# Evictions as a stream of their own, one unit behind their matmuls, in a two-block transformer kernel

## The reference, cut to what matters

```python
# first block, 2 layers, 256 tokens
h = rmsnorm(x, norm_w); proj = h @ w_in            # 1024 -> 4360 columns
ya = softmax_attention(8 heads, causal, ALiBi) * silu(ag)
yb = head_norm(retention(4 heads, rotated q, k)) * silu(bg)
yc = head_norm(mlstm(4 heads, chunks of 128) * sigmoid(co)) * silu(cg)
x = x + concat(ya, yb, yc) @ w_out
...
# second block, 2 layers, x (256 tokens) and a context (256 tokens), 9 modulation vectors
x = x + 0.5 * m[2] * swiglu(modulate(rms_norm(x), m[0], m[1]), w_ffn1)      # and the context
z = modulate(rms_norm(x), m[3], m[4]) @ w_in                                # and the context
ya, yb = neighborhood_attention(6 heads), window_attention(6 heads, 2 kv)   # local and context keys
yc = silu(layer_norm(depthwise_conv(31 taps)))
x = x + m[5] * ((g0 * ya @ w_out_a + g1 * yb @ w_out_b + g2 * yc @ w_out_c) @ w_out)
x = x + 0.5 * m[8] * swiglu(modulate(rms_norm(x), m[6], m[7]), w_ffn2)      # hidden width 2816
```

## Time and profile before

| | |
|---|---|
| median of 3 runs | 2630.19 us (2627.18 to 2636.57) |
| the profiled execution | 2638.58 us, span 2636.8 us |
| PE busy | 2457.2 us, 93% of the span |
| DVE busy | 1600.4 us, 61% |
| ACT busy | 877.7 us, 33% |
| mean granted clock of PE | 0.945 of full speed |

### The profile page before, as it was taken

One profiled execution on the slowest core, in us unless ns is written; L12 is line 12 of the kernel. 1 busy time (PEld: TensorE's weight loads), 2 busy tenths in 40 slices (PEclk: granted clock), 3 DMA queues, 4 the chain that ended last, 5 costly groups with the idle time before them and its releaser, 6 DMA issues.

```text
span 2636.8 us, 33057 instructions
## 1 busy us (share of the span) xinstructions
PE 2457.2 (93%) x13210; PEld 2077.3 (79%) x13210; DVE 1600.4 (61%) x2950; ACT 877.7 (33%) x1488; POOL 222.6 (8%) x321
## 2 busy tenths in 40 slices
PE   5888887799999999989989999989999999998998
PEld 5777776688888876668888888888888887788998
DVE  3875875577767445554458986654443345665665
ACT  3343433322222333333332222232222234344443
POOL 1000000100001200001111111100000020011000
PEclk9898987799999897999989999989999989798999
DMA  6533542254444310112325655522322232134553
GB/s 227 180 121 104 175 136 72 75 173 168 168 167 152 96 62 22 37 54 86 101 80 192 237 210 203 191 85 88 100 93 95 96 104 84 52 121 152 183 184 122
DMA packets 95353, 332.99 MB, mean 126 GB/s; under 512 B 11040, under 2 KB 13216, under 8 KB 94816
## 3 DMA queue, kind: packets, MB, share of 16 engines
q1 hardware_dynamic: 70496, 244.41, 27.2%
q0 software_dynamic: 23376, 84.80, 10.0%
q10 hardware_dynamic: 1328, 1.66, 0.2%
HBM read 329.78 MB, written 2.48 MB: 126 GB/s over the span
## 4 chain that ended last, share of the span: by engine, by line
PE 77%; DVE 13%; ACT 5%; issue 3%; POOL 1%; DMA 1%; ACTq 0%; POOLq 0%; DVEq 0%
PE PS L417 76%; DVE WL L1083 3%; ACT WH L794 2%; DVE ST L1096 1%; DVE NT L1092 1%; PE PS L720 1%; ACT P L795 1%; DVE AR L1093 1%; DVE JK L1093 1%; DVE HL L1092 1%; DVE PJ L1092 1%; DVE CV L1092 1%; ACT PT L794 1%; POOL SS L1672 1%; DMA CST<-in_cst 0%
## 5 line engine op out<-in xcount | busy, mean ns | idle before, releaser
L417 PE MATMUL PS<-HH,WH 128*128 128x512 f32 (+1 forms) x2136 | 772.3, 362 | 21.7 <-DVE HL L1092 21.4
L1083 DVE TENSOR_TENSOR WL<-RAW,WH 128x1024 fp32r<-128x1024 f32 (+2 forms) x482 | 575.4, 1194 | 324.7 <-ACT WH L794 323.6
L417 PE MATMUL PS<-HL,WH 128*128 128x512 f32 (+1 forms) x2136 | 758.9, 355 | 0.0
L417 PE MATMUL PS<-HH,WL 128*128 128x512 f32 (+1 forms) x2136 | 758.8, 355 | 0.0
L794 ACT ACTIVATE WH<-RAW 128x1024 fp32r<-128x1024 f32 (+2 forms) x482 | 490.4, 1019 | 247.5 <-PE PS L417 247.5
L417 PEld LDWEIGHTS PS<-HH,WH 128*128 128x128 f32 x2136 | 415.1, 194 | 95.1 <-DVE HL L1092 28.6
L417 PEld LDWEIGHTS PS<-HL,WH 128*128 128x128 f32 x2136 | 416.0, 195 | 56.4
L417 PEld LDWEIGHTS PS<-HH,WL 128*128 128x128 f32 x2136 | 415.2, 194 | 56.8
L417 PE MATMUL PS<-GH,WH 128*128 128x512 f32 (+1 forms) x776 | 270.8, 349 | 0.0
L417 PE MATMUL PS<-GH,WL 128*128 128x512 f32 (+1 forms) x776 | 270.7, 349 | 0.0
L417 PE MATMUL PS<-GL,WH 128*128 128x512 f32 (+1 forms) x776 | 270.5, 349 | 0.0
(11 more groups left out here) (219 smaller groups left out, 3125.1 us busy)
## 6 DMA issues: line engine op xcount, KB each, us to landing
RAW<-in_wst SPq DMA_DIRECT2D x420, 512.0 KB, 3.5
AR<-in_w_adaT POOLq DMA_DIRECT2D x144, 512.0 KB, 3.7
RAW<-in_wst SPq DMA_DIRECT2D x48, 384.0 KB, 3.0
BM<-rpb_rows POOLq DMA_DIRECT2D x48, 64.0 KB, 2.6
CB<-in_cc POOLq DMA_DIRECT2D x2, 1024.0 KB, 9.9
RAW<-in_wst SPq DMA_DIRECT2D x8, 256.0 KB, 2.7
RAW<-in_wst SPq DMA_DIRECT2D x4, 396.0 KB, 5.3
rpb_rows<-in_rpb POOLq DMA_DIRECT2D x2, 697.5 KB, 10.0
```

The lines of the kernel that those rows point to most:

```text
L417: return e.matmul(o, l, r, start=start, stop=stop)
L1083: return e.tensor_tensor(out=o, in0=a, in1=b, op=op)
```

## The change

Four things change. (1) Evictions leave the D stream and become a stream V of their own on ACT, DVE and POOL. (2) A dense unit is written in two halves on PE; D therefore stands twice as often in `order` and the other streams are mixed between halves. ACT and DVE do `high` and `low` at the first half and nothing at the second. (3) The V step of unit e is put right after the first half of unit e+1, so behind the `high` and `low` of that step; a mark "F", and the first step of each norm, bring all evictions of finished units at once. (4) `boundary` has a new order written in halves, and the last M steps of a layer's projections stand behind an F.

```diff
@@ mix
     for name, n in steps.items():
+        if name == "D":
+            n *= 2
         out += [((2 * i + 1) / (2 * n), name) for i in range(n)]
@@ plan, first block
-        order += mix(D=2, A=3, M=4)
+        order += mix(D=2, A=3, M=2) + ["F", "M", "M"]
@@ boundary
         if last:
-            return ["D", "N", "D", "N", "N", "N", "N", "D"] + ["N"] * 5 + ["D"]
-        return ["N", "N", "D"] + mix(D=1, N=8) + ["D"] * HELD
+            return ["D", "N", "D", "D", "N", "N", "D"] + ["N"] * 2 + ["D"] + ["N"] * 3 + ["D", "N", "N", "D"]
+        return ["N", "D", "N", "D", "N", "N", "D", "N", "N", "D", "N", "N", "D", "N", "N"] + ["D", "D"] * HELD
@@ mixer
-        out += mix(B=nb - b0, P=4, C=9)
+        out += ["F"] + mix(B=nb - b0, P=4, C=9)
@@ plan, end
-    B = ["D"] * HELD
+    B = ["D", "D"] * HELD
...
+    out, dense, left, norm = [], 0, 0, 0
+    for name in order:
+        if name == "F" or name == "N" and norm % 10 == 0:
+            while left < dense // 2:
+                out.append("V")
+                left += 1
+        norm += name == "N"
+        if name == "F":
+            continue
+        out.append(name)
+        if name == "D":
+            dense += 1
+            if dense % 2 and left < dense // 2:
+                out.append("V")
+                left += 1
+    order = out + ["V"] * (len(S) - left)
@@ tensor_program, dense
+                todo = [(j, k) for j in range(len(x.tiles)) for k in range(un.kt)]
-                for j, d in enumerate(x.tiles):
+                for y, (j, k) in enumerate(todo):
+                    d = x.tiles[j]
+                    if y == len(todo) // 2:
+                        yield
@@ scalar_program (vector_program alike, with low(u); pool_program's dense() becomes evictions())
         def dense():
-            silu = [0]
             for u in range(NS):
                 high(u)
+            for x in S:
+                for u in x.split:
+                    high(u)
+                yield
+                yield
+
+        def evictions():
+            silu = [0]
             for e_ in S:
                 un = U[e_.u]
-                for u in e_.split:
-                    high(u)
                 for d in e_.tiles if un.last else ():
```

More of the change, by code:

```diff
@@ L465, in dense @@
                 u, un = x.u, U[x.u]
+                todo = [(j, k) for j in range(len(x.tiles)) for k in range(un.kt)]
                 wh = WH[:, u % NS, 0:un.kt * un.cols].rearrange("p (k c) -> p k c", c=un.cols)
                 wl = WL[:, u % NS, 0:un.kt * un.cols].rearrange("p (k c) -> p k c", c=un.cols)
-                for j, d in enumerate(x.tiles):
-                    if un.first:
+                for y, (j, k) in enumerate(todo):
+                    d = x.tiles[j]
+                    if y == len(todo) // 2:
+                        yield
+                    if k == 0 and un.first:
                         released(T[d].before)
-                    if j == 0:
+                    if y == 0:
                         q.wait_ge(*ad.at("wh", u))
@@ L474, in dense @@
                     P = PS[T[d].bank]
[L475 to L488, removed]
+                    a, z = un.first and k == 0, un.last and k == un.kt - 1
+                    c = slice(128 * j, 128 * j + 128)
+                    if un.mode == "f":
+                        xh, xl = operand(un, k, T[d].halves)
+                        m = T[d].cols
+                        mm(P[:, 0:x.n], wh[:, k, c], xh[:, m], a, False)
+                        mm(P[:, 0:x.n], wh[:, k, c], xl[:, m], False, False)
+                        i = mm(P[:, 0:x.n], wl[:, k, c], xh[:, m], False, z)
+                    else:
+                        xh, xl = operand(un, k, range(x.n // 2))
+                        mm(P[:, 0:un.cols], xh[:, c], wh[:, k, :], a, False)
+                        mm(P[:, 0:un.cols], xl[:, c], wh[:, k, :], False, False)
+                        i = mm(P[:, 0:un.cols], xh[:, c], wl[:, k, :], False, z)
+                    if k < un.kt - 1:
+                        continue
                     if x.closes and d == x.tiles[-1]:
@@ L1075, in scalar_program @@
         q.wait_ge(d_cst, 32)
-        return dict(D=dense(), N=norm(), M=mlstm(), T=retention(), A=attention1(), B=attention2(), L=lnorm(), E=ada())
+        return dict(D=dense(), N=norm(), M=mlstm(), T=retention(), A=attention1(), B=attention2(), L=lnorm(), E=ada(), V=evictions())
     def vector_program(e):
@@ L1109, in dense, with evictions @@
         def dense():
-            silu = [0]
             for u in range(NS):
                 low(u)
+            for x in S:
+                for u in x.split:
+                    low(u)
+                yield
+                yield
+        def evictions():
+            silu = [0]
             for e_ in S:
                 un = U[e_.u]
-                for u in e_.split:
-                    low(u)
                 for d in e_.tiles if un.last else ():
@@ L1664, in vector_program @@
         return dict(D=dense(), N=norm(), M=mlstm(), T=retention(), A=attention1(), B=attention2(), P=rope(), C=conv(),
-                    L=lnorm(), E=ada(), K=misc())
+                    L=lnorm(), E=ada(), K=misc(), V=evictions())
     def pool_program(e):
@@ L1683, in add, with evictions @@
             gn.same("ss", j, i, halves[-1])
-        def dense():
+        def evictions():
             for e_ in S:
@@ L1783, in misc @@
                 yield
-        return dict(D=dense(), N=norm(), M=mlstm(), T=retention(), L=lnorm(), E=ada(), K=misc())
+        return dict(V=evictions(), N=norm(), M=mlstm(), T=retention(), L=lnorm(), E=ada(), K=misc())
     def sync_program(e):
```

## The result

The changed kernel is slower: 2648.1 us (median of 6 runs, 2644.4 to 2653.8) against 2634.8 (6 runs of the kernel before, 2627.2 to 2644.6). The ratio is 1.005, interval 1.0026 to 1.0075. The forecast was 2614.7. The direction is wrong. The time lies near the edge of the range, and nearest to the third rival, "late evictions decide" (2657). The profiled execution has a span of 2652.0 us, 15.2 more than before.

The account below looks back on a forecast made before the run. PE, busy 93% of the span, was taken as the bound, so only its idle or half-clock time could be won. Gains of -47 and losses of +31.5 us gave net -15.5, to 2614.7 us; 8-in-10 range 2582 to 2650.

Parts of the forecast that it names:

- late evictions decide: Rival: high and low before every eviction stall PE at all counted places, 69 us plus 5 against 47; 2657 us, chance 0.17.
- gain 1: Attention and mLSTM of block one: halves cover PE's waits on ACT and DVE; -20 us, half of a 40 us ceiling.
- gain 2: Start of each layer: reordering frees little of 10.6 us idle because DVE is busy; -4 us for two layers.
- gain 3: Mixers, attention with gates and branches: halves cover the waits; -14 us of a 27 us ceiling, bounds -4 and -25.
- gain 4: Four boundaries around mixers and feed-forward parts: two DVE waits go; -9 us, bounds +6 and -20.
- loss 1: Down projections, 12 places: the last operand slice comes later, behind high and low; +9 us, bounds 4 and 28.
- loss 2: Two-tile units at o0 and o1: second half awaits a bank evicted late; +4, +2 and +3, sum +9, bounds 3 and 20.
- loss 3: Around the 4-tile unit v2: banks are evicted late, behind high; +6.5 us, bounds 3 and 9.
- loss 5: Switching: some 50 more breaks of the dense stream at 0.1 us each; +5 us, bounds 2 and 10.
- Cover is enough: Rival: nearly all idle time and half clock in block one's attention and the mixers goes; 2577 us, chance 0.15.
- DVE's load decides: Rival: DVE works through the same list, so waits only move; gains 25, losses 28, 2627 us, chance 0.17.
- The clock swings: Rival: small matmuls between halves pull PE's clock down, mixer stretches to 0.80; 2659 us, chance 0.04.

Follow-up runs that it names:

- old_mm: tm_whole with the last mix before the output projection as in the kernel before (no F, no two M steps in a row); ratio 0.9847, 2598.8 us.
- pairs_now: Changed kernel, but only o0 and o1 units evicted right behind themselves, other evictions one unit behind; ratio 0.9980 to the kernel before, 2632.5 us.
- v_now: Changed kernel with each eviction right behind its own unit's second half, so halves without lag; ratio 0.9893 to the kernel before, 2613.6 us.
- whole: Changed kernel with dense units whole again where steps are mixed; evictions stay one unit behind; ratio 1.0077 to the kernel before, 2663.0 us.
- whole_now: v_now with whole dense units in the mixes, so no lag and no halves there, new boundary order kept; ratio 0.9929 to the kernel before, 2620.7 us.
- experiment 6: The run whole_now, 2620.7 us; its table sets whole units or halves against evictions one unit behind or at once, by spans: 2662.0, 2652.0, 2621.2, 2615.2 us.
- tm_whole: v_now with whole units only in block one's mixes with mLSTM, retention and modulation steps; ratio 0.9825 to the kernel before, 2594.3 us.
- after_tm: Changed kernel, lag kept, with whole units only in the mixes of mLSTM, retention and modulation steps; ratio 0.9992 to the kernel before, 2636.6 us.
- w_second: Changed kernel with high and low moved from a unit's first half to its second; ratio 0.9905 to the kernel before, 2616.5 us.
- old_boundary: v_now with the boundary order of the kernel before, each dense unit there as two halves in a row; ratio 0.9968 to the kernel before, 2631.7 us.

## Why the prediction was wrong

The terms of the sum, with what the profile after shows for each:

| term | predicted | measured |
|---|---|---|
| gain 1, attention of block one | -20 | -18.2, of it -11.3 the shift into `o1`: -7 |
| gain 2, start of each layer | -4 | +4.0 |
| M and T stretches | not in the sum | +13.1 |
| gain 3, mixers | -14 | about -11 |
| gain 4, boundaries | -9 | -11.8 |
| loss 1, down projections | +9 | +6.6 |
| loss 2, units with two tiles | +9 | +25.7, of it +10.0 the shift: +15.7 |
| loss 3, `v2` | +6.5 | about +10 |
| loss 4, output projections | +2 | +3.4 |
| loss 5, switching | +5 | nothing apart |

The shift is taken from old_mm, so from kernels without the lag. The measured terms sum to +21.8. The span at the last dense unit is 15.8 us later, so some 6 us were won elsewhere; 3.8 of these right behind `o0`, in places of 28.7 and 44.9 us before, 26.9 and 42.9 after.

Four steps make most of the gap between forecast and result: M and T (13), gain 1 (13), gain 2 (8) and loss 2 (7).

**Loss 2 failed at `o1`.** The step was "at `o1` A steps cover most, +3". They cover nothing of it: the timeline shows E's passes, `low` and then X in one row of DVE's list, 5 us behind the unit. I had taken the timeline of the pair from rows without any other stream, and assumed that other streams on PE give the eviction time; they also stand ahead of it on DVE. The lag is worth 11.6 to 13.0 of the 20.6 us there: without it `o1` goes to +9.0 in pairs_now and to +7.6 in v_now, and `o0` from +5.2 to -4.3 in pairs_now. The rest is about the size of the shift by the two M steps behind F (10.0 in old_mm). With 25.7 us the two-tile units lie above the bound of 20, without the shift inside it. For `o0` the mechanism was right, and the size too (+5.2 of +6).

**Gain 1 was a third of the forecast, and its cause was misread.** I took half of a ceiling of 40 us, of which 15 were half clock. The waits of A for PT fell by 7.6 us (14.3 to 6.7), about the 7 that are left beside the shift. But they are 5.8 us in whole, which has the lag and whole units, 8.8 in v_now, which has halves and no lag, and 13.2 in whole_now, which has neither. So either of the two shortens them, and the sign I had named for a right forecast (PT from 31 to about 15 us) came while the stretch with `o1`, which should have lost 7 to 10 us in the first layer, gained 4. What the halves win in attention, `o1` and `o0` together is 15 to 19 us, by the table of experiment 6; the lag costs 19 to 22 in the same places. The clock gave nothing: the stretch up to `o1` has 0.85 in both layers, where it had 0.92 and 0.80.

**The M and T stretches were never costed.** I looked for time where PE idled and so left out the stretch in which it idled 0.5 us of 56.6. There was nothing to win there, but something to lose. Gain 2 failed too, +4.0 for -4: PE waits 4.1 us in each layer for the copy PJ on ACT, an eviction, where it had no such wait. Without the lag, halves cost 5.5 us at the start (v_now) and whole units nothing (tm_whole, whole_now within 0.3). With the lag, whole units still stand at +1.3 in whole and +3.0 in after_tm, so how the +4.0 divides between halves and lag stays open. In M and T with halves the stream of dense matmuls is broken 17 times instead of 11 in each layer (a break is small matmuls of other streams between two dense ones). The times from the start of the last dense matmul before a break to the start of the first after it sum up to 23.1 us instead of 17.0, and that is the whole of the loss in the first layer; 10 of the 112 small matmuls in them came from the stretch behind. PE's waits there are 3.7 us instead of 0.3: for MI, WL and PJ. whole, tm_whole and after_tm, with whole units, are within 0.2 us of before there, in place of +5.9. Why a break costs so much here is settled only in part: those waits are 3.4 of 6.1 us, and w_second, with evictions and weights ordered otherwise, has 20.7 us in the same 17 breaks. In the mixer the breaks go from 20 to 37 and their time falls from 132.2 to 125.7 us. So loss 5, a price per break, is the wrong form. I read it so: a break is free where PE would have waited for ACT or DVE anyhow, and costs where it never waited.

**Gain 3 was right**, a little smaller than forecast; the waits of B for PT, 16.6 us before, are 7.3 with halves and 14.1 in whole, so there it is the halves that shorten them. whole_now against tm_whole, 2620.7 and 2594.3 us, shows what halves in attention and mixers bring when neither lag nor M and T stand in the way: 27 us by the ratios (0.9929 to 0.9825), 24 by the spans.

**Gain 4 was right.** The whole of it is the order (old_boundary). I had reckoned that the late `high`, `low` and X eat part of the gain, and they do: 7.0 us, from -18.8 to -11.8. In the kernel after PE waits 4.3 to 5.0 us for SQ, the square of the late X, in each boundary; in v_now it waits 0.8 us at the same boundary before a feed-forward part. **Losses 1, 3 and 4** had the right mechanism. The size was right for 1 and near for 4; 3 came out above its upper bound of 9. PE waits for GL 6 times, not 12, and at most 1.4 us; the three at 256 columns take 1.2 to 1.4, where I had worked out 1.1 and 1.4. Without the lag the loss at the down projections is gone: PE waits for no GL in v_now.

**The rivals.** "Late evictions decide" is nearest to what happened: the lag costs 37 us in all against the 26.5 that I counted and the 42 from which I said it would decide. The threshold was too high, since the gains were smaller than the 47 it stood against and the halves' cost in M and T (13.1) came on top. I gave it 0.17, less than a third of the forecast's chance, because I let every loss be small at its lower or middle estimate. "Cover is enough" and "DVE's load decides" don't fit: PT waits halved (30.9 to 14.0 us), as the forecast said. Two of their sums need a word: the 53 us of "cover is enough" hold only with the 4 us of gain 2, which its line doesn't name, and gains of 25 against losses of 28 give 2633 for "DVE's load decides", not 2627. "The clock swings" didn't come at the size that I gave it: taking the granted clock as a mix of the two levels, in the changed kernel (1 - 0.948) x 2 = 10.4% of 2652 us, 276 us, are at the lower level of 1.2 GHz, before 11%, 290 us, and the best kernel, tm_whole, at 0.955 has 234 us. The two windows of the mixer, kernel before and after:

```profile
934.50:1013.70 79.20, 77.70 (x363) 56.09 (x361) 39.84 (x72) 29.28 (x56) 0.00 (x0) 1.00 0.17 55
1013.70:1179.60 165.90, 151.29 (x667) 108.85 (x667) 100.39 (x259) 59.77 (x160) 0.00 (x0) 0.87 0.11 36
```

```profile
960.40:1040.30 79.90, 77.34 (x358) 54.80 (x357) 35.97 (x70) 29.40 (x58) 0.00 (x0) 0.98 0.15 50
1040.30:1192.00 151.70, 144.85 (x655) 102.30 (x654) 99.82 (x257) 57.80 (x157) 0.00 (x0) 0.89 0.11 36
```

The second stretch, 14 us shorter, holds gain 3, and its clock went from 0.87 to 0.89. In M and T the breaks did cost some clock. With 17 breaks the granted clock of this stretch was 1.00 in 5 profiled stretches and 0.97 in 7 (two layers of six kernels); with 11 breaks it was 1.00 in all 12. At 0.97 some 5 to 6% of 63 us are at the lower level, which costs 2 us at most, and the stretches at 1.00 lost 3.6 to 5.9 us all the same. The Trainium skill, "TensorE: Matmul & The Clock Gate", section "A second HAM failure mode: psum-queue depth-cycling", from which this rival came, is so borne out in direction in these stretches, by 0.03 of the clock; over the whole kernel the mean clock rose, from 0.945 to 0.948.

## What to carry to other kernels

Where every engine walks one written order, an eviction belongs ahead of the next unit's weight preparation, since both wait for the same matmul and here the preparation is the one that can wait: PE's waits for WL are 15 to 22 us in the changed kernel and in the three without it. Three ways to do that were each worth 1.5% against the changed kernel, and 16 of 509 steps carried half of it. Cutting dense units to fill another stream's waits pays where PE waits (24 to 27 us here) and costs where it doesn't (18 to 19 us): cost the stretches that have nothing to win as well. A hand-made order at a border can be tested by itself, and was worth 18.7 us without the lag, with halves in the mixes (18.3 at the boundaries with whole units), while with it the boundaries are 11.8 us shorter. A wait that gets shorter is no proof of the cause that was thought of: PE's waits for PT in block one fell with the lag alone and with the halves alone.

## What the runs showed of the hardware that was not expected

In the first layer of the kernel after PE kept the full granted clock of 1.00 over 62.4 us with 17 breaks and 3.8 us of idle time, its waits at most 1.9 us each; in the second, with the same breaks, it was 0.97 over 63.6 us. An E pass of 128x1024 (1.22 us) and `low` (1.23 us) follow each other on DVE at 1.14 to 1.15 us, less than the duration of either.
